# Second attention block: split scores of two heads in 64-row halves, longer leads for scores and turned q and k, a new order of the projections

## The reference, cut to what matters

```python
h = rms_norm(x, norm_g);  proj = h @ w_in          # 4*384 + 4*384 + 2*256 columns
a_q, a_k, a_v, a_g, b_q, b_k, b_v, b_g, m_q, m_g = split(proj)
qa = rope(rms_norm(heads(a_q), g0)); ka = rope(rms_norm(heads(a_k), g1))   # 6 heads of 64
oa = softmax(causal(qa @ ka.T / 8)) @ heads(a_v)
qb, kb = the same with b_q, b_k                                            # 6 heads of 64
ob = softmax(qb @ kb.T / 8 + log(count of dilated patterns)) @ heads(b_v)
om = softmax(rms_norm(m_q) @ rms_norm(k_mem).T / 8) @ v_mem                # 4 heads, 256 memory keys
x = x + concat(oa * silu(a_g), ob * silu(b_g), om * silu(m_g)) @ w_out
```

## Time and profile before

| what | value |
|---|---|
| time, median of 3 runs | 1688.66 us (1687.91 to 1690.15) |
| the profiled execution, its own time | 1690.31 us |
| its span, first to last instruction | 1688.5 us |
| busy share of the span: PE, DVE, ACT, POOL | 96%, 60%, 43%, 3% |
| block 2 of the first layer | about 1085 to 1360 us |
| its 44 steps of attention | 1157.7 to 1334.4 us |
| block 2 of the second layer | about 1402 us to the end |

### The profile page before, as it was taken

How to read it: one execution, slowest core, us unless ns; L and a number is a source line. 1 busy time by engine, 2 the same in 40 slices (tenths; PEclk the granted TensorE clock), 3 DMA queues, 4 the chain that set the end, 5 groups by cost and what they waited for, 6 DMA issues and landing times.

```text
span 1688.5 us, 21496 instructions
## 1 busy us (share of the span) xinstructions
PE 1618.3 (96%) x8009; PEld 1326.6 (79%) x8009; DVE 1005.9 (60%) x2246; ACT 729.7 (43%) x1503; POOL 57.8 (3%) x80
## 2 busy tenths in 40 slices
PE   6999999999999999999999999999989999998999
PEld 6878777788887878777788887999767789985667
DVE  4597656444444397757443344486876554788663
ACT  4444443333234443543332434434456553354662
POOL 0000002000001000002000001000000010000000
PEclk9999999999999999999999999999999999999999
DMA  6332121323323223112233323332112233211121
GB/s 219 93 92 71 42 63 51 100 88 100 100 94 96 85 87 88 51 50 63 76 96 92 99 90 110 104 88 60 57 38 69 76 95 92 83 56 38 38 76 62
DMA packets 80883, 136.23 MB, mean 81 GB/s; under 512 B 8190, under 2 KB 33420, under 8 KB 80780
## 3 DMA queue, kind: packets, MB, share of 16 engines
q1 hardware_dynamic: 77264, 129.48, 25.7%
q10 hardware_dynamic: 3516, 5.37, 1.0%
HBM read 132.74 MB, written 2.10 MB: 80 GB/s over the span
## 4 chain that ended last, share of the span: by engine, by line
PE 46%; DVE 13%; ACT 4%; issue 2%; POOL 0%; ACTq 0%; DVEq 0%
PE gemm_bank L695 35%; PE aux_bank L762 3%; PE aux_bank L791 3%; DVE w_lo L1343 2%; PE aux_bank L779 2%; DVE rope L1442 1%; DVE head_sums L1395 1%; ACT w_hi L1021 1%; DVE probs L1498 1%; ACT probs L1068 1%; DVE kT L1482 1%; PE aux_bank L750 1%; DVE probs L1510 1%; ACT L1296 0%; PE aux_bank L939 0%
## 5 line engine op out<-in xcount | busy, mean ns | idle before, releaser
L1021 ACT ACTIVATE w_hi<-raw 128x512 fp32r<-128x512 f32 (+3 forms) x524 | 305.5, 587 | 673.3 <-PE gemm_bank L695 671.9
L1343 DVE TENSOR_TENSOR w_lo<-raw,w_hi 128x512 fp32r<-128x512 f32 (+3 forms) x524 | 329.9, 636 | 441.9 <-ACT w_hi L1021 440.2
L695 PE MATMUL gemm_bank<-act_hi,w_hi 128*128 128x512 f32 x768 | 316.7, 412 | 10.9 <-DVE mq_flat L1383 3.7
L695 PE MATMUL gemm_bank<-act_hi,w_lo 128*128 128x512 f32 x768 | 300.2, 391 | 0.0
L695 PE MATMUL gemm_bank<-act_lo,w_hi 128*128 128x512 f32 x768 | 299.9, 391 | 0.0
L695 PE MATMUL gemm_bank<-w_hi,act_hi 128*128 128x384 f32 (+3 forms) x736 | 269.3, 366 | 6.4 <-DVE bq L1383 2.9
L695 PE MATMUL gemm_bank<-w_lo,act_hi 128*128 128x384 f32 (+3 forms) x736 | 257.2, 349 | 0.0
L695 PE MATMUL gemm_bank<-w_hi,act_lo 128*128 128x384 f32 (+3 forms) x736 | 257.2, 349 | 0.0
L695 PEld LDWEIGHTS gemm_bank<-act_hi,w_hi 128*128 128x128 f32 x768 | 144.6, 188 | 47.9 <-issue 12.7
L695 PEld LDWEIGHTS gemm_bank<-act_lo,w_hi 128*128 128x128 f32 x768 | 144.8, 189 | 31.9 <-issue 2.9
L695 PEld LDWEIGHTS gemm_bank<-act_hi,w_lo 128*128 128x128 f32 x768 | 144.5, 188 | 31.0
(11 more groups left out here) (289 smaller groups left out, 2132.7 us busy)
## 6 DMA issues: line engine op xcount, KB each, us to landing
raw<-in_w_in SPq DMA_DIRECT2D x104, 512.0 KB, 3.5
raw<-in_w_in SPq DMA_DIRECT2D x64, 384.0 KB, 3.3
raw<-in_w_out SPq DMA_DIRECT2D x32, 512.0 KB, 3.7
raw<-in_w_branch SPq DMA_DIRECT2D x24, 512.0 KB, 3.7
raw<-in_w_mem_kv SPq DMA_DIRECT2D x8, 512.0 KB, 3.8
raw<-in_w_in SPq DMA_DIRECT2D x16, 256.0 KB, 2.8
raw<-in_w_in SPq DMA_DIRECT2D x8, 416.0 KB, 4.8
x<-in_x SPq DMA_DIRECT2D x4, 512.0 KB, 5.2
```

The costliest lines, as they stand in the source:

```text
L695: last = pe.matmul(o, a, c, start=begin and n == 0, stop=end and n == 2)
L1021: act.activation(w_hi[:, s % RING, 0:n], raw[:, p % RAW, kk % PIECE, 0:n], ACT.Copy)\
L1343: dve.tensor_tensor(w_lo[:, s % RING, 0:n], raw[:, p % RAW, kk % PIECE, 0:n], w_hi[:, s % RING, 0:n].bitcast(F32), ALU.subtract).then_inc( ...
```

## The change

- The groups are projected in the order aq, ak, bq, bk, av (then bv, mq, ... as before). ACT evicts bq and bk, and av after it. DVE no longer evicts bq.
- ACT squares the eight b tiles beside the eight slabs of av, and DVE sums them there; the rest of the b norm goes on in the attention, two pieces a step, as before.
- A turned q or k is split into hi and lo: ACT rounds the bank to `q_hi`, `k_hi` (`turned_hi`), DVE subtracts to `q_lo`, `k_lo` (event `low`). No copies of q and k with zeroed halves are left, nor POOL's memset. The `low` event stands one step after the turn, after `scale` and before `scores` in the list of DVE.
- Scores of a unit of block 2 are six fp32r products: for each of hi*hi, lo*hi, hi*lo one for head 0 on rows 0 to 63 and one for head 1 on rows 64 to 127, into banks 0 and 1, alternating.
- Units 0 and 1 of a causal pair, and each two units of a memory pair, have their scores together in the two banks, with one hand-over.
- Scores begin four steps ahead where a buffer is free (four `probs` buffers, not three). In the attention they stand at step 0 (units 2 and 3), and then at 2, 4, 6, 8 and so on, at even steps only, up to 40.
- Turns stand at steps 0, 5, 11, 17, 23, 29 and 34; `low` at 1, 6, 12, 18, 24, 30 and 35. The first pair is turned at slab 3 of av, its `low` is at slab 4, the scores of units 0 and 1 at slab 5 (before: slab 4 of bk, and units 0 and 1 at slabs 5 and 6).

```diff
@@ class Stream
                 self.begin[mine[0]].insert(0, ("scale", m))
-                if mine[0] >= 2:
-                    self.begin[mine[0] - 2].append(("scores", m))
+                if mine[0] >= 2 and self.together(m):
+                    last = max(self.together(m)) - self.buffers
+                    free = self.steps_of[last][-1] + 1 if last >= 0 else 0
+                    self.begin[max(mine[0] - SCORES_LEAD[block], free, 0)].append(("scores", m))
             self.fill(fill, weight)
+        def together(self, m):
+            if self.block == 1:
+                return {m: 0}
+            kind, i = self.kind(m), m % NT
+            if kind.name == "memory":
+                return {} if i % 2 else {m: 0, m + 1: kind.n_keys(i) * P}
+            return {0: {m: 0, m + 1: P}, 1: {}}.get(i, {m: 0})
@@ def turn_at
             self.begin[step].append(("turn", g, x))
+            if self.block == 2:
+                at = [event[0] for event in self.begin[step + 1]].index("scores") \
+                    if "scores" in [event[0] for event in self.begin[step + 1]] else len(self.begin[step + 1])
+                self.begin[step + 1].insert(at, ("low", g, x))
@@ def attention_2
-        a.lead = {4: [("turn", 0, 0)], 5: [("scores", 0)], 6: [("scores", 1)]}
-        for g, (at_pair, step) in {1: (0, 1), 2: (0, 3), 3: (2, 1), 4: (2, 3), 5: (3, 3), 6: (4, 3), 7: (5, 3)}.items():
+        a.lead = {3: [("turn", 0, 0)], 4: [("low", 0, 0)], 5: [("scores", 0)]}
+        for g, (at_pair, step) in {1: (0, 0), 2: (0, 5), 3: (1, 5), 4: (2, 5), 5: (3, 5), 6: (4, 5), 7: (5, 4)}.items():
@@ PE
+        def scores_2(a, m):
+            g, kind = m // NT, a.kind(m)
+            if m % NT == 0:
+                aux_wait_read(pe, a.key("q", g, 0))
+                aux_wait_read(pe, a.key("k", g, 0))
+            banks = [aux_open(a.key("S", m, x), S_BANKS[x]) for x in range(2)]
+            for mm, c in a.together(m).items():
+                i, keys = mm % NT, kind.n_keys(mm % NT) * P
+                for n, (qq, kk) in enumerate(((q_hi, k_hi), (q_lo, k_hi), (q_hi, k_lo))):
+                    for x in range(2):
+                        r = slice(x * HD, (x + 1) * HD)
+                        last = pe.matmul(banks[x][:, c:c + keys], qq[r, g % 2, i * P:(i + 1) * P],
+                                         kk[r, g % 2, 0:keys], start=n == 0, stop=n == 2)
+                        if n == 2 and mm == max(a.together(m)):
+                            last.then_inc(full_of(a.key("S", m, x)), 1)
-            for name in ("ak", "av", "bq"):
+            for name in ("ak", "bq", "bk"):
...
-            gemm_led(gi_of(2, l, "bk"), "tokens", a, lambda kk: None)
+            gemm_led(gi_of(2, l, "av"), "tokens", a, lambda kk: None)
@@ ACT
+        def turned_hi(a, g):
+            for what, hi in (("q", q_hi), ("k", k_hi)):
+                bank = aux_wait_full(act, a.key(what, g, 0))
+                n = T if what == "q" else a.pairs[g][0].k_tiles * P
+                act.activation(hi[:, g % 2, 0:n], bank[:, 0:n], ACT.Copy).then_inc(turned_hi_ready, 1)
@@ DVE, turned
+            for n, (what, hi, lo) in enumerate((("q", q_hi, q_lo), ("k", k_hi, k_lo))):
+                key = a.key(what, g, 0)
+                columns = T if what == "q" else a.pairs[g][0].k_tiles * P
+                dve.wait_ge(turned_hi_ready, 2 * a.turn_count(g) - 1 + n)
+                dve.tensor_tensor(lo[:, g % 2, 0:columns], aux_bank[aux_place[key][0]][:, 0:columns],
+                                  hi[:, g % 2, 0:columns].bitcast(F32), ALU.subtract).then_inc(read_of(key), 1)
@@ DVE, block_2
-            alongside(a_heads, [gi_of(2, l, n) for n in ("av", "bq")], 2, at_end)
+            alongside(a_heads, [gi_of(2, l, n) for n in ("bq", "bk")], 2)
             for kk in range(KD):
                 for event in a.lead.get(kk, []):
-                    begin(a, *event)
-                split.beside(gi_of(2, l, "bk"), kk)
+                    if event[0] != "turn":
+                        begin(a, *event)
+                split.beside(gi_of(2, l, "av"), kk)
+                next(b_heads, None)
```

More of the change, by code:

```diff
@@ L138, in plan_groups @@
         two("ak", WA, WA)
[L139 removed]
         two("bq", 4 * WA, WB)
         two("bk", 4 * WA + WB, WB)
+        two("av", 2 * WA, WA)
         two("bv", 4 * WA + 2 * WB, WB)
@@ L754, in scores @@
             (g, i), kind = a.units[m], a.kind(m)
+            if a.block == 2:
+                scores_2(a, m)
+                return
             n_keys = kind.n_keys(i)
@@ L778, in turn_probs @@
                     c = (x * (j1 - j0) + j - j0) * P
-                    last = pe.transpose(bank[:, c:c + P], probs[a.where][m % 3][:, x, j * P:(j + 1) * P], ident[:, :])
+                    last = pe.transpose(bank[:, c:c + P], probs[a.where][m % a.buffers][:, x, j * P:(j + 1) * P], ident[:, :])
             last.then_inc(full_of(key), 1)
@@ L1074, in attention @@
                 split_beside(split, a, n, evict_beside)
+                for event in a.begin[n] if a.block == 2 else ():
+                    if event[0] == "turn":
+                        turned_hi(a, event[1])
                 for event in a.begin[n] + a.middle.get(n, []):
@@ L1273, in block_2 @@
             for n, _ in enumerate(head_squares(kind_tiles("a"), sq_2)):
-                split.beside(gi_of(2, l, "av"), n // 2)
-            evict(gi_of(2, l, "av"), ACT.Copy, lambda b: flat_2("av")[:, b, :])
-            split.through(gi_of(2, l, "bq"))
-            a = attention_2(l)
-            gi = gi_of(2, l, "bk")
-            split.beside(gi, 5)
-            exponentials(a, 0)
-            split.beside(gi, 6)
-            exponentials(a, 1)
-            evict(gi, ACT.Copy, lambda b: flat_2("bk")[:, b, :])
+                split.beside(gi_of(2, l, "bq"), n // 2)
+            for name in ("bq", "bk"):
+                evict(gi_of(2, l, name), ACT.Copy, lambda b: flat_2(name)[:, b, :])
             wait_gemm_read(act, gi_of(2, l, "bq"))
@@ L1286, in block_2 @@
             b_squares = head_squares(kind_tiles("b"), sq_2)
+            a = attention_2(l)
+            gi = gi_of(2, l, "av")
+            for kk in range(KD):
+                split.beside(gi, kk)
+                if kk == 3:
+                    turned_hi(a, 0)
+                if kk == 6:
+                    exponentials(a, 0)
+                next(b_squares, None)
+            evict(gi, ACT.Copy, lambda b: flat_2("av")[:, b, :])
             m_squares = head_squares([mq_tok[:, t, :, :] for t in range(NT)]
@@ L1467, in begin @@
         def begin(a, what, *of):
-            if what == "turn":
+            if what in ("turn", "low"):
                 turned(a, *of)
@@ L1475, in turned @@
         def turned(a, g, x):
-            kind = a.pairs[g][0]
-            bank = aux_wait_full(dve, a.key("q", g, x))
-            dve.tensor_copy(a.qT_of(g, x), bank[0:kind.rows, :]).then_inc(read_of(a.key("q", g, x)), 1)
-            bank = aux_wait_full(dve, a.key("k", g, x))
-            for hh in range(kind.group):
-                r = slice(hh * kind.d, (hh + 1) * kind.d)
-                ins = dve.tensor_copy(a.kT_of(g, x + hh)[r, 0:kind.k_tiles * P], bank[r, 0:kind.k_tiles * P])
-                if hh == kind.group - 1:
-                    ins.then_inc(read_of(a.key("k", g, x)), 1)
-                else:
-                    mark(ins)
+            if a.block == 1:
+                bank = aux_wait_full(dve, a.key("q", g, x))
+                dve.tensor_copy(a.qT_of(g, x), bank[0:QK, :]).then_inc(read_of(a.key("q", g, x)), 1)
+                bank = aux_wait_full(dve, a.key("k", g, x))
+                dve.tensor_copy(a.kT_of(g, x), bank[0:QK, :]).then_inc(read_of(a.key("k", g, x)), 1)
+                return
@@ L1491, in scores @@
-            keys = kind.n_keys(i) * P
-            if m >= 3:
-                aux_wait_full(dve, a.key("T", a.steps_of[m - 3][-1]))
+            kind, units = a.kind(m), a.together(m)
+            if max(units) >= a.buffers:
+                aux_wait_full(dve, a.key("T", a.steps_of[max(units) - a.buffers][-1]))
             for x in range(2):
-                c = a.column(m) + x
                 key = a.key("S", m, x)
                 bank = aux_wait_full(dve, key)
-                dve.tensor_tensor_reduce(out=probs[a.where][m % 3][:, x, 0:keys], in0=bank[:, 0:keys],
-                                         in1=kind.mask(i), scale=-kind.scale, scalar=3.0e38, op0=ALU.add, op1=ALU.min,
-                                         accum_out=neg_max[:, c:c + 1]).then_inc(read_of(key), 1)
+                for mm, b in units.items():
+                    c, keys = a.column(mm) + x, kind.n_keys(mm % NT) * P
+                    ins = dve.tensor_tensor_reduce(out=probs[a.where][mm % a.buffers][:, x, 0:keys],
+                                                   in0=bank[:, b:b + keys], in1=kind.mask(mm % NT), scale=-kind.scale,
```

(8 more changed lines are left out.)

50 lines of the change are left out of this document (24 added, 26 removed).

## The result

The changed kernel takes 1700.45 us (median of 4 runs, 1700.30 to 1700.87) against 1688.71 for the kernel before on the same chip: ratio 1.0069, 95% interval 1.0052 to 1.0086. It is slower by 12 us, where I forecast 1674.5. The profiled execution took 1700.87 us with a span of 1699.1, so 10.6 us more span than before.

What follows compares the result with a forecast made beforehand. PE's products and waits were taken to bound block 2. Per layer, scores -10.0, `low` +12.0, step 0 +2.8, probabilities +0.5, gone -10.0, bq -1.7 gave -6.4; with clock, -14 in two layers: 1674.5 us, range 1651 to 1692.

Steps and rivals of the forecast that it cites:

- What bounds the kernel: Block 2: PE, busy 96%, sets the time; product time removed is worth up to its length, a wait its full length.
- Scores: Block 2's scores as six fp32r products a unit on row halves: 10 us a layer saved from 32.7.
- two cases of overlap: Scores' halves overlap with weight loads one after another, gain 8.1 us a layer, or with loads overlapped too, gain 15.1.
- that rule: Changing tiling mode drains the engine: 22 score calls cost 7 us a layer, not 3.3; 1683 us, within a 0.15 chance.
- The wait at `low`: PE's scores at steps 6, 12, 18, 24, 30 wait for DVE's low halves: 12.0 us a layer, mean 2.4.
- the slower rival: Waits at `low`, steps 6 to 30, average 4.5 us: kernel slower by 8 us, 1697; decides from 3.7 us; chance 0.11.
- Step 0: Two scores and a turn in a row on banks 0 and 1 wait for DVE's maxima: 2.8 us a layer.
- The waits for probabilities: PE's waits for DVE's scaled probabilities in attention: 6.0 + 0.8 us a layer go, 0.5 put back.
- The clock: Early attention steps at the lower clock: fewer clustered waits may save half the time, 1 us a layer.
- The order of projections: ACT evicts bq with time to spare, so PE's wait ahead of the attention goes: 1.7 us a layer with its drain.
- Gone or new: PE's waits for turned k (2.4 us) and bq (1.5) go; those for mq, bv and `probsT` (1.0, 0.8, 1.5) stay.
- my -7.0: Forecast change per layer: -6.4 us from the terms, plus 1 us saved by the clock; -14 in two layers.

Runs made afterwards that it cites:

- the run with two filled waits: Changed kernel with idle products put into two of PE's waits, 8 before step 0's second scores and 16 before step 6's scores: 1698.24 us, ratio 1.0055.

## Why the prediction was wrong, step by step

**What bounds the kernel** was right: PE's products and waits set the time, and each wait costs its length. It costs more than that where the clock falls after it, which I did not carry through.

**Scores** were right in size, -10.0 against -12.0 a layer, but by another road. I placed the value between two cases of overlap. The runs show the full overlap (products 1.90 a causal pair) with a dearer entry: 0.3 us a call and not 0.15. The Trainium skill, "TensorEngine Tiling (Array Packing)", section Key Properties, says both, that tiles load and multiply in parallel and that a change of mode drains the engine; the passes of 0.12 us and the 0.3 us a call agree with it, though no run here separates a drain from other costs of entering the form. At 22 calls that is near the 7 us that I had written for that rule, against 3.3 in my sum.

**The wait at `low`**: 12.0 forecast, 13.0 and 13.1 measured, with step 6 the longest. In the first layer steps 6, 12, 18, 24 and 30 have 5.4, 1.3, 1.2, 2.6 and 1.9 us, for my 4.0, 1.8, 1.0, 2.8 and 2.4; the rest, 0.6, is at step 1. The mean, 12.4 / 5 = 2.5 us, is under the 3.7 from which the slower rival decides. So that rival was not what happened, though its sign was.

**Step 0**: 2.8 forecast, 3.3 and 2.0 measured as waits. Its price in time was larger: with the low halves on the turn's own step, the turn there cost 9.3 us in two layers, through what it delays and the clock. The trace of the changed kernel shows one such delay. At step 1 ACT had been idle for 7.08 us until PE was done with a slab of the ring, DVE then for 4.42 us until ACT's `w_hi`,

```profile
1166.01 0.56 DVE L1401 TENSOR_TENSOR w_lo<-raw,w_hi 128x384 fp32r<-128x384 f32 x1 [4.42 <-ACT w_hi L1064]
```

and only after that and a chain of roots did DVE scale the probabilities, for which PE waited 1.96 us. The kernel before has no wait for probabilities there.

**The waits for probabilities** are the step that failed: I let 6.0 + 0.8 go and put 0.5 back; they are 9.9 and 9.5 us. I had named the cause myself, DVE late with its own queue, and then counted on it to be less busy. One of them, at step 16, first in the kernel before and then in the changed one:

```profile
1236.78 0.66 PE L779 MATMUL aux_bank<-ident,probs 128*128 128x128 f32 x4 [1.95 <-DVE probs L1510]
```

```profile
1238.58 0.75 DVE L1453 TENSOR_REDUCE head_sums<-sq 128x4 f32<-128x256 f32 x2 [1.86 <-ACT sq L1084]
...
1239.77 0.17 DVE L1472 TENSOR_SCALAR head_sums<-head_sums 128x24 f32<-128x24 f32 x1
...
1242.37 0.43 DVE L1464 TENSOR_TENSOR mq_flat<-mq_flat,head_rstd 128x256 f32<-128x256 f32 x1
1242.71 0.16 DVE L1570 RECIPROCAL row_inv<-row_sum 128x2 f32<-128x2 f32 x1
1242.90 0.88 DVE L1574 TENSOR_SCALAR probs<-probs,row_inv 128x512 f32<-128x512 f32 x2
...
1243.84 0.66 PE L822 MATMUL aux_bank<-ident,probs 128*128 128x128 f32 x4 [2.06 <-DVE probs L1574]
```

The exponentials of these rows had begun at 1224.82 and 1225.53, and were over by 1226.3, sixteen microseconds before DVE scaled them: it was at the roots, which belong to the norm of the memory queries (`mq_flat`). The same roots stand ahead of the 1.95 us of before. What did go there are the copies of the turned q and k, 2.1 us of DVE, and they were replaced by idle time: DVE stood for 1.86 us until ACT's squares, and ACT had the exponentials of the two joined units (1235.73 to 1237.67) ahead of them. So less work for DVE gained nothing, since DVE waits in its queue for ACT. This is read from two traces; no run takes the squares alone elsewhere. Beginning scores earlier can't help, as `scale` keeps its place in the queue; from a lead of two to four the wait rose from 5.2 to 7.5 us. Faster scores alone left it at 5.8 us. With the new places of the turns it was 9.9.

**The clock**: I took 1 us a layer off at most; it cost about 4.5. Rows 2 had shown 0.97 in the early steps, and I had treated it as a thing that fewer waits would mend, not as one that more waits could multiply.

**The order of projections** gained more than its 1.7 us: 5.9 us in two layers, by mq as well (2.7 us in the second layer).

**Gone or new**: bq and turned k went as forecast, mq and bv too, which I had let stand (2.7 us a layer); `bgT` came with 0.7. Per layer the misses are scores -2.0, `low` +1.0, probabilities +9.2, the drains of 1.8 that I had also taken off, mq and bv -2.7, bgT +0.7, turned q, `probsT` and step 0 together -0.9, clock +5.1: 12.2 of the 12.3 us between my -7.0 and the measured +5.3.

What stays open: half of the 4.7 us of the shorter lead among the changed turns, and the clock's price: 0.33 comes from one row of the table, the run with two filled waits shows 0.2 to 0.3, and executions of one kernel 0.45. No run isolates what ACT's squares cost.

## What to carry to other kernels

A wait on one engine's late queue isn't mended by starting its inputs earlier: look at when the input was ready (here 16 us before), whether the late step moves in its queue, and what the late engine itself waits for there. Place a step that frees a bank where the work behind it on the waiting engine doesn't need that bank; one step's difference for the same two subtractions made 25.9 us of waits a layer out of 3.6, and 13.0 out of 1.3. And where the waiting engine's clock falls after some of its waits, price a new wait above its own length, here by 0.2 to 0.45 us for each microsecond that runs at the lower clock.

## What was unexpected of the hardware

Two fp32r products on the two 64-row halves pass in the time of one at every width from 128 to 512 keys (0.11, 0.12, 0.17 and 0.23 us for two heads), with the loads hidden. A call costs some 0.3 us beyond its products (0.25 at 128 keys, 0.31 at 512), so at 128 keys the new form (0.58) is slower than fp32 on padded keys (0.45), and at 512 it saves 0.72 of 1.72 us.

PE's granted clock fell to 1.2 GHz after waits far shorter than the longest, and not after all of the same length. In the changed kernel it fell after 2.5 + 0.8 us at 1156 to 1161, after 2.0 us at 1171, and within the 5.4 us that end at 1194.5. In the first layer it did not fall after single waits of 1.5 us at 1232 and 2.6 at 1274, but in the second layer it did after the same two waits (at 1552 and 1594). So the length of a wait does not tell here whether the clock falls behind it. Once down, it stayed so while PE was again at work: in the 5 us from 1160 PE is busy 89% and the clock 0.66.

```profile
1160.00:1165.00 5.00, 4.44 (x19) 4.30 (x20) 1.59 (x5) 0.00 (x0) 0.00 (x0) 0.66 0.19 52
```
